# Layer 0's context output products worked inside the first expert tile, with a ring of six rows for gathers up to slot 144

## What is computed

```python
def _layer(x, xc, mod, mod_c, rows, last, ...):
    ...                       # norm, one input projection, three token-mixing branches
    x = x + gt1 * mix(p, o, rows)                       # mix(...) ends in "@ w_out"
    x = x + gt2 * peer(_rms(x, norm2) * (1 + sc2) + sh2)
    if not last:              # context tokens: layer 0 only
        xc = xc + cgt1 * mix(pc, oc, None)
        xc = xc + cgt2 * peer(_rms(xc, norm2) * (1 + csc2) + csh2)
    return x, xc

def _peer(h, wq, keys, u_tab, v_tab):       # per token: 8 heads x 16 experts of 16384
    ...                                     # eid, gw: expert numbers and softmax weights
    act = gelu(einsum("tkd,td->tk", u_tab[eid], h))
    return einsum("tk,tkd->td", gw * act, v_tab[eid])
```

## Time and profile before

| | us |
|---|---|
| median of 3 runs | 4367.65 (4362.76 to 4370.74) |
| the profiled execution, whole | 4369.42 |
| its span, first to last instruction | 4367.4 |
| mix_out of layer 0, first product to the last half row added | 554.8 to 664.3 |
| first dot of the first expert tile | 665.8 |
| first dot of the second expert tile | 993.7 |
| first dot of layer 1's expert tiles | 3063.2 |

### The profile page before, as it was taken

How to read it: one execution, slowest core, us unless ns; L and a number is a source line. 1 busy time by engine, 2 the same in 40 slices (tenths; PEclk the granted TensorE clock), 3 DMA queues, 4 the chain that set the end, 5 groups by cost and what they waited for, 6 DMA issues and landing times. The chain is left out here.

```text
span 4367.4 us, 55136 instructions
## 1 busy us (share of the span) xinstructions
PE 3697.2 (85%) x18945; PEld 1905.5 (44%) x18945; DVE 3006.2 (69%) x6251; ACT 1721.1 (39%) x5272; POOL 1647.7 (38%) x1508
## 2 busy tenths in 40 slices
PE   7998998988888888888886788889898888887777
PEld 3566854433433433433432334775443343343222
DVE  3964567876776775875875886457797687687444
ACT  2223623444344344344342454343444433433333
POOL 0004503444443444444443442352444444444332
PEclk9999999999999999999998999899999999999999
DMA  8360159999999999999999998014999999999997
GB/s 340 117 243 26 37 198 372 421 420 420 410 416 422 410 420 419 409 419 421 407 417 366 408 388 305 2 37 180 418 421 421 421 419 421 421 408 421 422 421 327
DMA packets 238985, 1506.07 MB, mean 345 GB/s; under 512 B 28433, under 2 KB 33617, under 8 KB 71153
## 3 DMA queue, kind: packets, MB, share of 16 engines
q0 software_dynamic: 184320, 1342.26, 74.6%
q1 hardware_dynamic: 54384, 160.28, 9.8%
HBM read 1490.32 MB, written 12.12 MB: 344 GB/s over the span
## 5 line engine op out<-in xcount | busy, mean ns | idle before, releaser
L2851 PE MATMUL ps<-low,pediag 128*128 128x512 f32 x2180 | 1066.0, 619 | 231.6 <-ACT pediag L2760 225.0
L2623 DVE CUSTOM_DVE_ANT_0 low<-low,hc 128x1024 f32<-128x1024 f32 x545 | 667.9, 1225 | 371.2 <-DMA low<-in_experts_dram,eid 356.0
L2602 POOL DMA_INDIRECT low<-in_experts_dram,eid x537 | 588.0, 1095 | 823.9 <-PE ps L2851 809.3
L2752 ACT ACTIVATE low<-peact 128x1 f32<-128x1 f32 x1152 | 232.0, 201 | 1389.7 <-DVE peact L2623 1388.5
L2851 PEld LDWEIGHTS ps<-low,pediag 128*128 128x128 f32 x2180 | 390.0, 193 | 835.6 <-ACT pediag L2760 514.4
L2760 ACT ACTIVATE pediag<-cst,low 128x128 f32<-128x128 f32 x1152 | 462.5, 401 | 42.5 <-PE ps L2851 5.1
L2755 ACT ACTIVATE low<-low,gw 128x1 f32<-128x1 f32 x1152 | 339.1, 294 | 37.4
L2851 PE MATMUL ps<-wide_a,pediag 128*128 128x512 f32 x640 | 307.2, 610 | 55.0 <-ACT pediag L2760 54.7
L2060 PEld LDWEIGHTS ps<-qkvT,arena 128*128 128x128 f32 x2560 | 315.6, 195 | 77.1 <-issue 77.1
L2851 PE MATMUL ps<-wide_b,pediag 128*128 128x512 f32 x640 | 302.8, 604 | 45.0 <-ACT pediag L2760 44.7
L2060 PE MATMUL ps<-qkvT,arena 128*128 128x128 f32 x2560 | 316.2, 277 | 2.4 <-ACT qkvT L2024 2.4
(11 more groups left out here) (502 smaller groups left out, 5779.8 us busy)
## 6 DMA issues: line engine op xcount, KB each, us to landing
pjdot<-in_mod_t_dram SPq DMA_DIRECT2D x64, 512.0 KB, 5.3
arena<-in_w_mod_dram SPq DMA_DIRECT2D x24, 1024.0 KB, 11.8
arena<-in_peer_wq_dram SPq DMA_DIRECT2D x8, 2048.0 KB, 17.1
low<-in_experts_dram,eid POOLq DMA_INDIRECT x609, 15.2
pjw<-in_w_cols_dram SPq DMA_DIRECT2D x18, 512.0 KB, 3.7
plw<-in_w_cols_dram SPq DMA_DIRECT2D x18, 512.0 KB, 8.2
qkvT<-mod_rows SPq DMA_DIRECT2D x9, 512.0 KB, 11.1
arena<-in_w_z_dram SPq DMA_DIRECT2D x2, 2112.0 KB, 12.4
```

Of the source, the lines that this page charges most:

```text
L2602: nc.gpsimd.indirect_dma_start(ring.row(g), None, table, bass.IndirectOffsetOnAxis(eid[:, j % 2, k:k + 1], 0)).then_inc(ring.landed(g), 16)
L2623: nc.vector.tensor_tensor_reduce(out=dot_out if final else ring.row(g)[:, 0:D], in0=ring.row(g)[:, 0:D], in1=hc[:, j % 2, :], scale=1.0, s ...
L2752: nc.scalar.activation(ge[:, g % 2, 0:1], act_v[:, j % 2, k:k + 1], ACT.Gelu_apprx_tanh).then_inc(gelu_ready, 1)
L2851: last = nc.tensor.matmul(ps[:, half, :], diag[:, g % DIAGS, :], ring.row(g)[:, D + half * 512:D + (half + 1) * 512], start=k == 0, stop=k ...
```

## The change

In layer 0 `mix_out` now makes the products of the four latent tiles alone (`HALVES` is 8). Its SP no longer loads the context rows, the context gate, and no longer stores context rows. The context tiles' four half products are made in `peer`, in the first tile: `w_out` is loaded again, in sixteen pieces of 128x512 (256 KB) into two halves of `dot_out`, each piece followed by two matmuls (one per context tile) into banks 2 and 3, at slots 40, 46, ... 82 for the first half and 94, 98, ... 122 for the second. DVE gates and adds at slots 85, 87, 124 and 126. The rows, their gate and a scratch row (256 KB each) stand in ring row 7, the tiles' `mixT` in ring row 4. So the ring has six rows until slot 144; rows 4 and 7 join at slots 149 and 152. POOL issues slots 0 to 6 in `mix_out`, not 0 to 8. The three element-by-element loads into `n1` move from the head of SP's list in `peer` to the end of these loads. Layer 1 is worked as before.

```diff
-    HALVES = 2 * len(tiles)
     EARLY = 4
+    HALVES = 2 * EARLY
...
+    W_AT, W_STEP, W_ADD = (40, 94), (6, 4), (85, 124)
...
+                def late_rows(half):
+                    sp.dma_start(late_row(0), mod_row(kit, L, 0, 2)[:, half_cols(half)]).then_inc(late_in, 16)
+                    for a, t in enumerate(late):
+                        sp.dma_start(late_row(1 + a), kit.ctx[0, t * P:(t + 1) * P, half_cols(half)]).then_inc(late_in, 16)
+                def late_store(half):
+                    sp.wait_ge(late_sum, 2 * half + 2)
+                    for a, t in enumerate(late):
+                        sp.dma_start(kit.x_d[t * P:(t + 1) * P, half_cols(half)], late_row(1 + a)).then_inc(late_stored, 16)
+                def late_piece_in(n):
+                    if n < 2:
+                        sp.wait_ge(sc.h_ready, 1)
+                    else:
+                        sp.wait_ge(late_used, n - 1)
+                    half, k = divmod(n, KD)
+                    sp.dma_start(piece_of(n), w_out_half(kit, L, half)[:, k, :]).then_inc(piece_in[n % 2], 16)
+                def late_loads():
+                    late_rows(0)
+                    for n in range(KD + 2):
+                        late_piece_in(n)
+                    late_store(0)
+                    for n in range(KD + 2, KD + 4):
+                        late_piece_in(n)
+                    sp.wait_ge(late_stored, 32)
+                    late_rows(1)
+                    for n in range(KD + 4, 2 * KD):
+                        late_piece_in(n)
                     for a, src in enumerate((kit.mod_d[L + 1, 1, D:2 * D], kit.mod_d[L + 1, 1, 0:D], kit.norm1[L + 1, :])):
                         sp.dma_start(n1[:, a, :], src.rearrange("(k p) -> p k", p=P),
                                      allow_slow_non_contiguous=True).then_inc(n1_in, 16)
+                    late_store(1)
+                    sp.wait_ge(late_stored, 64)
...
+                    if late and i == 0:
+                        late_loads()
...
-                for g in range(ring.size + 1, SLOTS * M):
+                for g in range(ring.begun, SLOTS * M):
...
-                    pool.wait_ge(summed, g - ring.size + 1)
+                    before = ring.used_by(g)
+                    if before is not None:
+                        pool.wait_ge(summed, before + 1)
+                    elif ring.at[g] == 7:
+                        pool.wait_ge(late_stored, 64)
+                    else:
+                        pool.wait_ge(late_used, 2 * KD)
...
+                def late_add(k):
+                    for half in range(2):
+                        a, odd = divmod(k - W_ADD[half], 2)
+                        if odd or not 0 <= a < 2:
+                            continue
+                        dve.wait_ge(late_in, 48 * (half + 1))
+                        dve.wait_ge(late_used, KD * (half + 1))
+                        n = 2 * half + a
+                        if n:
+                            dve.wait_ge(late_sum, n)
+                        nc.vector.tensor_tensor(late_row(3), ps[:, 2 + a, :], late_row(0), ALU.mult).then_inc(late_gated, 1)
+                        dve.wait_ge(late_gated, n + 1)
+                        nc.vector.tensor_tensor(late_row(1 + a), late_row(1 + a), late_row(3), ALU.add).then_inc(late_sum, 1)
...
+                def late_products(k):
+                    for half in range(2):
+                        n, off = divmod(k - W_AT[half], W_STEP[half])
+                        if off or not 0 <= n < KD:
+                            continue
+                        if n == 0 and half == 0:
+                            pe.wait_ge(sc.hT_ready, 1)
+                        elif n == 0:
+                            pe.wait_ge(late_gated, 2)
+                        at = half * KD + n
+                        pe.wait_ge(piece_in[at % 2], 16 * (at // 2 + 1))
+                        for a, t in enumerate(late):
+                            last = nc.tensor.matmul(ps[:, 2 + a, :], mixT[:, n, t, :], piece_of(at),
+                                                    start=n == 0, stop=n == KD - 1)
+                        last.then_inc(late_used, 1)
...
+SHORT_UNTIL = 144
...
-                ring = RowRing(first_row, rows, [5, 6, 2, 3, 4, 0, 1, 7], sems[0:RING + 1])
+                ring = RowRing(first_row, rows, [5, 6, 2, 3, 4, 0, 1, 7], sems[0:RING + 1], [5, 6, 2, 3, 0, 1], SHORT_UNTIL)
```

More of the change, by code:

```diff
@@ L2177, in mix_out @@
     s0 = int(tiles[0] >= NC)
-    turns = [i for i in range(1, n_tiles) if (tiles[i] >= NC) != (tiles[i - 1] >= NC)]
     with ExitStack() as mem, phase(nc, kit, "gates_in", "x0", "x1", "sum_sq", "root_sq", "y_ready",
@@ L2216, in products_reading @@
                 return 1
-            here = [i for i in range(n_tiles) if tiles[i] // 2 == row - 4]
+            here = [i for i in range(EARLY) if tiles[i] // 2 == row - 4]
             return 2 * (max(here) + 1) if here else 1
@@ L2251, in _ @@
                     load_wq(sp, part)
-                for i in range(2, n_tiles):
+                for i in range(2, EARLY):
                     store(sp, i - 2)
@@ L2405, in add @@
                         dve.wait_ge(x_in[i % 2], 16 * (i // 2 + 1))
[L2406 removed]
+                        dve.wait_ge(gates_in, 16)
                     dve.wait_ge(prod_ready, q + 1)
@@ L2452, in _ @@
                 pool.wait_ge(turned, n_tiles)
-                for g in range(ring.size):
+                early = min(ring.begun, ring.size)
+                for g in range(early):
                     if g:
-                        pool.wait_ge(prod_ready, products_reading(ring.order[ring.place(g)]))
+                        pool.wait_ge(prod_ready, products_reading(ring.at[g]))
                     nc.gpsimd.indirect_dma_start(
@@ L2458, in _, with peer @@
                         bass.IndirectOffsetOnAxis(kit.eid[:, 0, g:g + 1], 0)).then_inc(ring.landed(g), 16)
-                for b in range(2):
-                    pool.wait_ge(stored[b], 16 * ((n_tiles - b) // 2 if n_tiles > EARLY else 1))
-                g = ring.size
-                nc.gpsimd.indirect_dma_start(
-                    ring.row(g), None, kit.experts.rearrange("l e d -> (l e) d"),
-                    bass.IndirectOffsetOnAxis(kit.eid[:, 0, g:g + 1], 0)).then_inc(ring.landed(g), 16)
-def peer(nc, kit, L, tiles, here, qkvT, ring, room, held, stored):
+                for g in range(early, ring.begun):
+                    for b in range(2):
+                        pool.wait_ge(stored[b], 16)
+                    nc.gpsimd.indirect_dma_start(
+                        ring.row(g), None, kit.experts.rearrange("l e d -> (l e) d"),
+                        bass.IndirectOffsetOnAxis(kit.eid[:, 0, g:g + 1], 0)).then_inc(ring.landed(g), 16)
+def peer(nc, kit, L, tiles, here, mixT, qkvT, ring, room, held, stored):
     N, M = len(tiles), here
@@ L2528, in peer @@
         steps = lambda i: range(SLOTS if i < M else R_AT + 1)
+        late = [] if final else [t for t in tiles if t < NC]
+        piece_in = (lw0, lw1)
+        piece_of = lambda n: dot_out[:, (n % 2) * 512:(n % 2 + 1) * 512]
+        late_row = lambda a: ring.rows[7][:, a * 512:(a + 1) * 512]
+        half_cols = lambda half: slice(half * 512, (half + 1) * 512)
         def mixed_rows(eng):
             for b in range(2):
-                eng.wait_ge(stored[b], 16 * ((N + 1 - b) // 2))
+                eng.wait_ge(stored[b], 32)
         with nc.Block(no_gpsimd_drain=bool(held)) as block:
@@ L2726, in _ @@
                             dot(g)
-                        if ahead and (i, k) == (0, 60):
+                        if ahead and (i, k) == (1, 20):
                             next_gain()
@@ L2734, in _ @@
                             late_piece(k)
+                        if late and i == 0:
+                            late_add(k)
                         if i < M and i + 1 < N:
@@ L2859, in piece @@
                             pe.wait_ge(n1_copied, j - 2)
+                        if late and j == 2:
+                            pe.wait_ge(late_gated, 4)
                         sc.turn_h(j)
@@ L2885, in _ @@
                             late_piece(k)
+                        if late and i == 0:
+                            late_products(k)
                         if i < M and i + 1 < N:
@@ L2990, in backbone @@
                         low[:, LOW_Y:LOW_Y + D], ring, sems[-2:])
-                peer(nc, kit, 1, order, len(order), qkvT, ring, low[:, LOW_Y:LOW], None, sems[-2:])
+                peer(nc, kit, 1, order, len(order), mixT, qkvT, ring, low[:, LOW_Y:LOW], None, sems[-2:])
 def constants():
```

46 lines of the change are left out of this document (22 added, 24 removed).

## The result

| | before | after |
|---|---|---|
| median of 8 runs, us | 4367.27 (4361.54 to 4373.73) | 4381.42 (4375.67 to 4384.91) |
| span of the profiled execution, us | 4367.4 | 4381.8 |
| after / before | | 1.0029 [1.0018, 1.0039] |

The changed kernel is slower by 0.29%, some 13 us with 8 to 17 in the interval. The forecast was 4381.

A forecast was written before the change was run, and what follows sets the result against it. Expert tiles were taken to run at the DMA engines' pace, 421 GB/s. Terms -23.4 + 17 + 5 + 17 - 2.5 = +13.1 took the profiled 4369.4 to 4382.5 us, so 4381 for the median; range 4364 to 4391.

The forecast's parts named there:

- Step 1: Head of the gather stream: slots 3 to 6 leave earlier without the last four half products in mix_out; gain 23.4 us.
- The rival that it would not start earlier: In mix_out, something the twelfth product hid could hold slots 3 to 6, removing the gain: 4404 us, chance 0.03.
- Steps 2 and 3: First tile: 26 added transfers in the gather stream cost 17 us, six rows and a fuller PE 5 us.
- the third term: First tile: six ring rows and PE's added products cost 5 us, between 0 and 12, at some five places.
- just enough: First tile with six rows: a gather has 7.9 us left where a lone one needs 7.3.
- The 4.4 us: The Trainium skill's figure for one gather, against 7.3 measured; with it the six-row term would be near 0.
- The second term: First tile's gather stream: 26 added transfers of 256 KB, 6.8 MB, cost 17 us.
- Step 4: Slot 136: third tile's row fetched late, behind stores queued after the `n1` loads; loss 17 us, 2.5 back in the hole.
- The rival that the row comes in time: Third tile's row: stores and fetch not held up by the `n1` loads, so no wait; 4366 us, chance 0.19.
- The rival that PE sets the pace: First tile, slots 40 to 98: PE cannot make up waits, so 12 us for 5; 4388 us, chance 0.12.
- the second tile's first dot: Sign: near 990 shows added bytes and six rows together; over 1000 means PE, under 986 that six rows cost nothing.

The follow-up runs named there:

- e3: Kernel before with six ring rows until slot 144, all products still in mix_out: 4374.87 us, ratio 1.0015 to before.
- e7: e2 with only two of sixteen pieces loaded and all but each half's first product 8 columns wide: 4360.00 us, ratio 0.9983 to before.
- e6: e2 with the context products one slot later, at odd slots, so none shares a slot with a query: 4364.76 us, ratio 0.9996 to before.
- e1: Changed kernel with the `n1` loads behind the fetch of the third tile's row and their use moved to slot 60: 4366.95 us, ratio 1.0002 to before.
- e2: Changed kernel with the third tile's row fetched ahead of all sixteen pieces, `n1` loads left in place: 4363.94 us, ratio 1.0000 to before.
- e5: e2 with all loads kept but all except each half's first product 8 columns wide: 4366.04 us, ratio 0.9998 to before.

## Why the prediction was right, and which terms were mis-sized

**Step 1 (-23.4): right.** Slots 3 to 6 left at once, 1.24 to 1.6 us apart, and slot 3 landed 23.3 us nearer to slot 2's gather (10.5 us behind it for 33.8). The same 23.4 at slot 32 is in part chance. Slot 8's landing is 18.9 nearer only: the 1 MB of row stores, which the prediction put there, and the loads behind them now land in that place (so their order says; no run has them alone). Among these are three loads of 512 KB that before landed between slots 24 and 32, behind the `n1` loads; there the kernel after takes 21.9 us for 25.6, which makes most of it good. The rival that it would not start earlier is out.

**Steps 2 and 3 (17 + 5): right in sum, wrong in both.** Together they took 22.3 by slot 128. But six rows alone took 8.8 (e3), the products 2.5 to 3.7, the 14 pieces 3.5 to 4.7. What is left when pieces and products are gone is 349.9 - (358.0 - 23.4) = 15.3 us (e7); less the 8.8 of e3 that is 6.5, by difference only: no run has it alone. The two remaining pieces and the context and gate rows' transfers would fit it (ten of 256 KB by slot 128, 6.2 us at 421 GB/s, an estimate). If they are it, and if e3's 8.8 holds beside the early start too, the third term was 11 to 12.5 and not 5, the second 10 to 11 and not 17.

The step that failed is "just enough" in the third, and it failed by where it was read. The prediction took gathers between 760 and 914 us and found that one which goes two issues later has 7.9 us left where a lone one needs 7.3. In that stretch e3 bears most of it out: slots 56 to 80 lose nothing, slots 48 to 56 1.3 us, and the worst place is where the prediction put it, with 3.5 us lost from slot 80 to 92 for the 2 predicted at slot 88. But six rows also cost 5.4 us in the first 40 slots, which the term left out. Slot 7's gather, which now waits for slot 1's sum, leaves 38.8 us behind slot 2's in e3 and not 32.5, and slots 3 to 8 lose 3.5 us; slots 32 to 40 lose 3.8 (between them 1.8 are made good). And e6 takes the crowding of product and query away for nothing. The 4.4 us that the prediction weighed against its 7.3, with a third term near 0, is out: the shortest landing of a gather in these traces is 5.4 us.

The second term is small for a like reason, as I read it. It priced every byte at 421 GB/s, as in a full stream; where a gather comes late the stream is not full, and a piece can land in the gap: 14 of them took 3.5 to 4.7 us where their price was 9.2 (14 of 26, of 17 us). No run shows the gaps filled; this is argued. That two errors met in 22 is luck, and e3 and e7 told it, not the time.

**Step 4 (17 less 2.5): right, in mechanism and size.** From the first `n1` load (963.09) to the row (1037.39) it took 74.3 us for the 71 predicted; ACT was idle 18.4; square to freed gather 9.04 us, predicted 9.0. Only the landing was shorter: slot 143's dot began 5.74 us after its gather, not 7.3. With that the hole is 15.7 by the prediction's own sum; the landings of slots 142 and 143 lie 18.2 us apart, which is 15.7 over their 2.5, and e1 and e2 put it at 14.8 and 16.1.

The rival that the row comes in time needed the stores not to be held up; they were, for 35.7 and 30.7 us, and in e1 another one for 60.1. The Trainium skill ("DMA: Bandwidth & Descriptors", section "Queues, rings and completion order") says that each DMA engine takes its descriptors in ring order. The trace agrees: e1's store behind the `n1` loads took 60.1 us, the fetch queued just ahead of them 7.9. The same section's other sentence, that completion is not first in, first out, gave no help here. The rival that PE sets the pace falls with e5: PE was busy 148.57 of 159 us after, and narrow products bring back 3.7 us of 22.

**The sum.** Predicted +13.1; in the ledger +17.0 at slot 160 and +15.8 at slot 639, of the medians +14.2 (8 to 17 by the interval). That the medians come nearer to the forecast than the ledger lies within the scatter: behind slot 639 the kernel before took 760.5 us to layer 1's first expert dot in its first profile, 755.4 in its second, and the kernel after 755.5. The bounds that the prediction gave for the second tile's first dot (990; over 1000 means PE, under 986 means free rows) were met: the dot came at 996.18, or at 992.6 without the 3.6 us by which this execution came later to slot 2's gather.

## What to carry to other kernels

When a stream of gathers is near the limit of the DMA engines, count the rows in flight before the bytes: two rows of eight cost more (8.8 us) than 14 loads of 256 KB put beside them (3.5 to 4.7), and giving one row back for 42 slots, with 768 KB of loads moved behind them, brought 3.6. Read the gathers over the whole stretch, its head too, before you say that fewer rows are enough: most of the cost lay in a few crowded slots and at the head. When work is moved in a hand-written queue, follow each transfer that now stands behind an element-by-element load, and put the one that somebody waits for ahead of it: 15 us of this change were the order of one fetch. And where two terms of a sum can trade against each other, the time can't tell them apart; run each alone.

## What the runs showed of the chip that was not expected

The DMA share hardly shows that a stream has gaps: 1.01 at 420 GB/s in the kernel before and 1.00 at 404, 402 and 399 GB/s in e3, after and e7, and still 0.98 in e3's short window at 378 (the windows above). Only the GB/s told them clearly apart.

A 4 KB load in single elements took 61.2 us to land beside gathers in one place, 62.7 in another and 60.0 before. The stream beside it went on almost at its pace: 409 GB/s in e1 from 1008 to 1064 us, with the loads on their way, where the kernel before has 419 in the same window. That is some 1.3 us of the 56 (an estimate from the two rates). What such a load costs most is the time of all that is queued behind it on the same queue.

Across a hole in the work the granted TensorE clock is 0.69, a mean between its two levels of 1.2 and 2.4 GHz, in the window from 1017 to 1055 us, and 1.00, the upper level, in the two windows ahead of it; PE had been idle 21.40 us of it. This added nothing that shows: the stretch from slot 160 to 639 took 1226.1 us after and 1227.3 before.
